# Expert weights of a block-sparse layer read row by row across the partitions, and tokens transposed in plain blocks

## What is computed

```python
t = modulate(rmsnorm(x, norm2_g), sh_m, sc_m)        # 512 x 1024
# a group of 4 is chosen, then 2 of its 8 experts; gates[e, t] are the weights
for e in range(32):
    a, u = split(t @ w_expert_in[e], 2)              # 1024 x 512
    y += ((silu(a) * u) @ w_expert_out[e]) * gates[e][:, None]   # 256 x 1024
x = rmsnorm(x + gt_m * y, final_norm_g)
```

## Time and profile before

| what | value |
|---|---|
| median of 3 runs | 1640.46 us |
| the profiled execution's own time | 1644.79 us |
| its span, from the first to the last recorded instruction | 1642.9 us |
| TensorE busy | 1461.7 us, 89% of the span |
| VectorE, ScalarE, GpSimd busy | 703.2, 378.8 and 316.9 us |
| mean granted clock of TensorE | 0.963 of full speed |
| moved by DMA | 232.59 MB, a mean of 142 GB/s |
| experts' loop on TensorE, first to last matmul | about 1379 to 1612 us |

### The profile page before, as it was taken

The page is one execution under the profiler, slowest core; times in us unless marked ns, Lnnn a source line. Parts: engine busy times, 40 slices in busy tenths (PEclk is TensorE's granted clock), DMA queues, the critical chain, the costliest instruction groups (busy, mean ns, idle before and its releaser), DMA issues. The chain is left out here.

```text
span 1642.9 us, 22231 instructions
## 1 busy us (share of the span) xinstructions
PE 1461.7 (89%) x8638; PEld 985.6 (60%) x8638; DVE 703.2 (43%) x1226; ACT 378.8 (23%) x799; POOL 316.9 (19%) x269
## 2 busy tenths in 40 slices
PE   5999999999999979989999999999989977888782
PEld 4864446884544457778888778673757764332220
DVE  5252344123369957775332144310354445332324
ACT  3224445104333333322100122301231010000001
POOL 3420021520007255534630000000000001111110
PEclk9999999999999979999999999999998978999996
DMA  5237110303112124414332040422033257999995
GB/s 186 81 121 237 52 54 24 103 26 128 52 52 77 59 71 130 131 52 168 127 129 77 0 129 26 73 72 67 22 123 111 95 204 310 425 421 426 422 378 219
DMA packets 119545, 232.59 MB, mean 142 GB/s; under 512 B 13329, under 2 KB 103023, under 8 KB 110483
## 3 DMA queue, kind: packets, MB, share of 16 engines
q1 hardware_dynamic: 114115, 220.54, 37.5%
q0 software_dynamic: 5184, 8.55, 1.4%
q10 hardware_dynamic: 144, 2.10, 0.3%
HBM read 223.65 MB, written 17.84 MB: 147 GB/s over the span
## 5 line engine op out<-in xcount | busy, mean ns | idle before, releaser
L962 PE MATMUL psv<-arena 128*128 128x256 f32 x1008 | 221.5, 379 | 2.1 <-issue 2.1
L962 PEld LDWEIGHTS psv<-arena 128*128 128x128 f32 x1008 | 191.1, 190 | 30.2 <-issue 4.4
L924 PE MATMUL psv<-arena,wslot 128*128 128x512 f32 x384 | 170.8, 598 | 1.8 <-DVEq L2214 1.8
L1634 ACT ACTIVATE arena<-pss 128x512 f32<-128x512 f32 (+1 forms) x157 | 84.8, 540 | 330.2 <-PE pss L924 276.3
L1549 PE MATMUL pss<-arena 128*64 128x512 f32 x432 | 118.0, 618 | 14.5 <-DMA arena<-w_expert_in 11.9
L924 PEld LDWEIGHTS psv<-arena,wslot 128*128 128x128 f32 x384 | 71.1, 190 | 85.5 <-issue 83.0
L924 PE MATMUL pss<-arena 128*128 128x256 f32 (+1 forms) x384 | 113.6, 453 | 5.8 <-ACTq L152 3.1
L2230 DVE TENSOR_TENSOR arena<-arena,psv 128x512 f32<-128x512 f32 x66 | 45.4, 687 | 163.5 <-PE psv L962 161.3
L2445 DVE SCALAR_TENSOR_TENSOR arena<-psv,ccols,arena 128x510 f32<-128x510 f32 (+1 forms) x96 | 71.9, 749 | 59.9 <-ACT arena L1801 56.8
L924 PEld LDWEIGHTS pss<-arena 128*128 128x128 f32 x384 | 71.7, 190 | 41.1 <-issue 28.4
L924 PE MATMUL psv<-wslot,arena 128*128 128x256 f32 x416 | 93.1, 385 | 3.0 <-DMA wslot<-w_in 2.6
(11 more groups left out here) (346 smaller groups left out, 2014.5 us busy)
## 6 DMA issues: line engine op xcount, KB each, us to landing
arena<-w_expert_in SPq DMA_DIRECT2D x27, 2048.0 KB, 26.8
wslot<-w_in SPq DMA_DIRECT2D x32, 1024.0 KB, 5.5
arena<-w_expert_out SPq DMA_DIRECT2D x32, 1024.0 KB, 27.3
wslot<-w_ada SPq DMA_DIRECT2D x18, 1024.0 KB, 5.4
arena<-w_in SPq DMA_DIRECT2D x10, 1024.0 KB, 6.8
wslot<-w_expert_in SPq DMA_DIRECT2D x5, 2048.0 KB, 21.5
arena<-w_ada SPq DMA_DIRECT2D x6, 1024.0 KB, 9.0
arena<-x SPq DMA_DIRECT2D x8, 512.0 KB, 7.9
```

The costliest lines, as they stand in the source:

```text
L924: m = mm(o, l, r, start=(n == 0), stop=(n == len(pairs) - 1))
L962: m = mm(o[:, j * HALF_T:(j + 1) * HALF_T], l[:, c, j * P:(j + 1) * P], r[:, c, :], start=new and j == 0 and c == 0, stop=j == 1 and c == ...
L1634: L.did(A(dst, src, func, **kw), s[sig] if sig else None, [s["free_s"]])
```

## The change

The two source views take rows p, p + 128 and so on into partition p. The pieces that are contiguous in memory are then one row each: 2 KB of `w_expert_in` (8 in a partition) and 4 KB of `w_expert_out` (2 in a partition). Bytes, number of loads and their order are as before. The transposes take plain blocks of 128 columns. Scale and shift are used where they already lie, in `gain` and `mod`, and `gsp`, `gs_dram`, their three transfers and the waits on `ld_gs` go.

```diff
-        gsp = sb("gsp", 2, KC)
...
-        gs_dram = scratch("gs_dram", 2, DM)
...
-        win_src = a["w_expert_in_2"][0].rearrange("(i x) (p c) n -> i x p c n", x=2, p=P)
-        wout_src = a["w_expert_out_2"][0].rearrange("(i x) (p c) n -> i x p c n", x=2, p=P)
+        win_src = a["w_expert_in_2"][0].rearrange("(i x) (c p) n -> i x p c n", x=2, p=P)
+        wout_src = a["w_expert_out_2"][0].rearrange("(i x) (c p) n -> i x p c n", x=2, p=P)
...
-            sp.dma_start(gs_dram[0, :].rearrange("(c p) -> p c", p=P), gain[:, 16:24],
-                         allow_slow_non_contiguous=True).then_inc(s["ld_gs"], 16)
-            sp.dma_start(gs_dram[1, :].rearrange("(c p) -> p c", p=P), mod[:, 24:32, 0],
-                         allow_slow_non_contiguous=True).then_inc(s["ld_gs"], 16)
...
-            sp.wait_ge(s["ld_gs"], 32)
-            load(gsp[:, :, :], gs_dram.rearrange("a (p c) -> p a c", p=P), "ld_gs")
...
-                    m = tr(o[:, c * P:(c + 1) * P], xg[:, k, h * 4 + c::KC], ident)
+                    m = tr(o[:, c * P:(c + 1) * P], xg[:, k, (h * 4 + c) * P:(h * 4 + c + 1) * P], ident)
...
-                    m = tr(o[:, c * P:(c + 1) * P], hid[:, k, c::2], ident)
+                    m = tr(o[:, c * P:(c + 1) * P], hid[:, k, c * P:(c + 1) * P], ident)
...
-            dve.wait_ge(s["ld_gs"], 48)
...
-                mul(o, by4(b), spread(gsp[:, 0, h * 4:h * 4 + 4]), s["free_v"])
-                add(o, o, spread(gsp[:, 1, h * 4:h * 4 + 4]), s["xe_ready"])
+                mul(o, by4(b), spread(gain[:, 16 + h * 4:20 + h * 4]), s["free_v"])
+                add(o, o, spread(mod[:, 24 + h * 4:28 + h * 4, 0]), s["xe_ready"])
```

More of the change, by code:

```diff
@@ L466, in build @@
             sprev_ready sc_ready o2_ready sq2_ready rt2_ready cat_ready x3_ready h3_ready lg_ready
-            lexp_ready ld_out win_used wout_used ld_gs yb_ready hidT_ready sil_ready hid_ready out_ready picked_ready icol_ready xn_saved x3_saved gla_used first_ready
+            lexp_ready ld_out win_used wout_used yb_ready hidT_ready sil_ready hid_ready out_ready picked_ready icol_ready xn_saved x3_saved gla_used first_ready
             table_ready index_ready xg_k0 xg_k1 xe_ready st_y0 st_y1
```

## The result

The changed kernel takes 1657.58 us at the median (1656.7 to 1658.5), the kernel before 1640.88 beside it. The ratio is 1.0107 with an interval of 1.0088 to 1.0125: 16.7 us slower. Measured a second time, on another occasion, it is 1657.41 against 1641.12, a ratio of 1.0097 (1.0082 to 1.0113). The forecast was 12.4 us slower, 1653. One execution of the kernel before, of 23 on that second occasion, took 3891.92 us; it has no profile here, and the ratios leave it out.

The account below looks back on a forecast made before the run. The prediction took the experts' loop to be bound by full DMA engines. Smaller pieces add 15.4 us, the earlier first gather returns 3, so 12.4 on the median 1640.46 gives about 1653 us; 8 in 10 range 1641 to 1664.

Parts of the forecast that it names:

- The bound: Experts' loop, 1386 to 1595 us: DMA engines are full, so longer transfers lengthen the kernel one for one.
- The price of a piece: Loop's weight loads: smaller pieces add 13.7 us for `w_expert_in` and 1.7 for `w_expert_out`, together 15.4 us.
- The line: DMA transfer time in full windows: 0.590 ns fixed per piece plus 2.372 ns per KB, for all 16 engines together.
- Rival (3): Loop: 2 KB pieces move as slowly as 1 KB in a full stream, +32.7 - 3, 1670 us; chance 0.09.
- rival (1): Loop: a piece's fixed price is small, a third, 5 to 6 us, less 3, giving 1643 us; chance 0.14.
- rival (2): Not slower: 2 KB pieces cost nothing and the gather comes 3.9 us early, 1636.6 us; chance 0.09.
- The credit for the gather: Before the loop: pair 0's gather lands sooner beside small pieces, gain 0 to 3.9 us, taken as 3.
- The tail: From the landing of pair 15's weights to the end of the span: 48.1 us, not changed.
- rival (4): TensorE's granted clock falls with waits and stays low at the tail, adding 3 to 10 us, 1659; chance 0.12.
- the forecast's own signs of being wrong: Loop still at 415 GB/s or more, loop at 360, or time from pair 15's weights to the end not 48 us.
- Costs at nothing: Issue of loads, removed small transfers (5 us at most without cover), VectorE's operands and transposes' stride cost or bring nothing.
- The marks: Profile after: 390 GB/s, first wait near pair 6, waits 25 to 30 us, 17.6 us a pair, gather near 1371.5.

Follow-up runs that it names:

- e_win: Changed kernel with the `w_expert_out` part undone: only `w_expert_in` is read row by row (2 KB pieces), `w_expert_out` keeps 8 KB; 1653.83 us, ratio 1.0076.
- e_8k: Kernel before with 4 neighbouring rows of `w_expert_in` in a partition (8 KB pieces), scale and shift read back by two small transfers; 1641.88 us, ratio 0.9995.
- e_4k: Kernel before with 2 neighbouring rows of `w_expert_in` in a partition (4 KB pieces), scale and shift read back by two small transfers; 1645.36 us, ratio 1.0021.
- e_1k: Against the kernel with only `w_expert_in` row by row: its rows cut in halves (1 KB pieces), each load issued as two; 1669.21 us, ratio 1.0169.
- e_two: Control, kernel before with each 2 MB load of `w_expert_in` issued as two of 1 MB (adjoining 8 KB pieces); 1642.76 us, ratio 1.0006.
- e_near2k: Kernel before, each `w_expert_in` load issued as two, neighbouring rows kept but written to places that don't adjoin (2 KB pieces); 1654.13 us, ratio 1.0076.

## Why the prediction was right, and where a term was off

**The bound.** Right: the loop is bound by the DMA engines, and added transfer time went one for one into the span (+14.04 in a difference of +13.8 in the table above; the other stretches nearly cancel). The share of 1.01 at 423 GB/s doesn't hold up to 1600, as the forecast read it: from 1550 to 1600 the kernel before shows 0.96 and 399, since its last weights land at 1594.77. No term rests on that. The loads ahead of the loop stayed hidden, as forecast: the engines' share in the changed kernel is 0.02 from 1378 to 1379, before pair 3's load at 1384.06.

**The price of a piece.** Right in kind, and 15.4 was 1.4 too much by the profile. The line, drawn from 1 KB pieces and the mix of 16 and 8 KB, held within some 2 us for the other mixes. Rival (3), the rate of 1 KB, fell with the 396 GB/s, rival (1) as well (it would have been 5 to 6 us), and so did rival (2), a change that isn't slower. The rule from the Trainium skill's page "DMA: Bandwidth & Descriptors", section "Why small descriptors are slow (HBM only)", gave an estimate near 6 us for the sum in the form in which the forecast used it (the 3 cycles alone), and 14.0 were measured. So these runs disagree with that estimate by more than a factor of two; a fixed cost per piece is there, but a larger one.

**The credit for the gather.** This is the term that failed most: "I take 3", on the reasoning that "Everything in the chain starts from this". The rows of pair 0 were there 2.15 us sooner after the gather's issue, `first` began 1.9 sooner, and the load of pair 3 was issued 0.68 us sooner (in `e_win` 0.35 later). What the forecast left out is the clock: TensorE had been idle, and `first`, which started sooner, ran 1.2 us longer, at 1.2 GHz for part of it. With 0.7 in place of 3, the sum would have been 14.7.

**The tail.** I had 48 us as unchanged and the clock as rival (4), "3 to 10 us". The tail took 49.83 us, so one of the forecast's own signs of being wrong came true, and rival (4) came in kind but below its lower edge: 1.70 us, of which 1.65 are `first` of pair 15 (8.74 instead of 7.09). It isn't certain in each kernel: `e_win` ran it in 7.09.

**The sum.** By the profiles it is 14.0 - 0.7 + 1.7 = 15.0, against 16.7 and 16.3 at the medians; the rest of 1.3 to 1.7 isn't explained; it is smaller than the 4.6 us by which the profiles differ ahead of the first gather. The forecast's 12.4 had a price 1.4 too high, a credit 2.3 too high and a tail 1.7 too short. That the first error offsets part of the other two is luck.

**Costs at nothing.** The transposes, eight at the full clock, take 1.09 us from plain blocks and 1.15 from every eighth column. There is a difference underneath that the forecast didn't look at, in the loads of the tile into TensorE that go before each matmul (PEld; busy us and mean ns of one, in the kernel before and the changed one):

```profile
L1543 PEld LDWEIGHTS psv<-const,arena 128*128 128x128 f32 x128 | 16.8, 197 | 22.1 <-issue 22.1
...
L1535 PEld LDWEIGHTS psv<-const,arena 128*128 128x128 f32 x128 | 15.0, 150 | 21.7 <-issue 20.6 <-DVE arena L2219 1.2
```

Every eighth column takes a mean of 197 ns to load, a plain block 150 (medians of 193 and 141). The matmuls hide nearly all of it: their medians are 276 and 273 ns. The small transfers: hidden to within some 2 us, in two measurements. SP's queue: "pieces don't lengthen an issue" was wrong with a full queue (10.66 us for two loads), and harmless, since the engines' share stays at 1.04 meanwhile.

**The marks.** 17.6 us a pair was exact. Waits of 25.8 us were within 25 to 30. The first wait came at pair 7, not 6. The gather's rows were there at 1371.2 for the 1371.5 named, but with luck: 1.26 us of that come from its earlier issue, which nothing in the forecast gave. "Up to 1360 nothing moves" was off by 1.3 us, which differs from kernel to kernel (the gather's issue lies between 1360.69 and 1365.29 in these profiles) and wasn't explained.

## What to carry to other kernels

Where a stretch is bound by the DMA engines, count pieces as well as bytes, and read the price of a piece from two windows with full engines and different sizes; here it was 0.5 to 0.6 ns over all 16 engines, which added under 1 us to a stretch of 209 with `w_expert_in` in 8 KB pieces and 12.3 us with 2 KB. Choose the order of rows so that a partition's bytes adjoin on both sides, and pay for it with strided transposes, whose longer loads were hidden here. Before counting a stall ahead of TensorE's work as a gain, look at what TensorE waits for next and at its clock: here most of the gain was lost to these two.

## What the runs showed of the hardware that I had not expected

A gather's time depends on the pieces that another queue moves meanwhile. Its median over all gathers was 10.4 us in the kernel before, 8.5 in `e_8k`, 8.0 in `e_4k`, 7.7 in `e_win` and 7.0 in the changed kernel. It doesn't fall further with 1 KB (8.2 in `e_1k`), and with 8 KB in twice as many loads it is 9.1 (`e_two`), so the size of the pieces isn't all of it. A transfer is cut where either side stops adjoining (`e_near2k`). And small pieces hold up SP's queue: two loads of 2 MB took 0.88 us of it with 128 pieces each (1420.76 before) and 10.66 with 1024 each (1421.09 after), both beside full engines; behind an empty queue the two kernels took 0.80 and 0.99 us (1386.00 and 1384.06). The windows show no idle engines for it.
